# Channel-major conv history, taps and y without turns on TensorE, and early conditioning slabs in twos

## What is computed

```python
mod = silu(c) @ w_ada + b_ada            # 9 conditioning rows, 6 x 2048 columns
h = rmsnorm(x, norm1_g) * (1 + scale1) + shift1
qa, ka, va, qb, kb, vb, r, glr = split(h @ w_in)
x = x + gate1 * merge_out(mix_a(qa, ka, va), mix_b(qb, kb, vb), r) @ w_out
h2 = rmsnorm(x, norm2_g) * (1 + scale2) + shift2
g_pre, u = split(h2 @ w_up)
gp = concatenate([state_conv, g_pre])    # 2 old rows for each sample, zeros for the prompt
conv = conv_b + conv_w[0]*gp[0:T] + conv_w[1]*gp[1:T+1] + conv_w[2]*gp[2:T+2]
y = x + gate2 * ((silu(conv) * u) @ w_down)
new_conv = gp[T:]                        # the last 2 rows, an output
```

## Time and profile before

| what | value |
|---|---|
| median of 3 runs | 1593.41 us (1593.29 to 1593.66) |
| span of the profiled execution | 1592.4 us |
| TensorE matmul busy | 1569.0 us, 99% |
| VectorE, ScalarE busy | 899.9 us, 665.7 us |
| DMA moved | 371.06 MB, mean 233 GB/s |

### The profile page before, as it was taken

The page is one execution under the profiler, slowest core; times in us unless marked ns, Lnnn a source line. Parts: engine busy times, 40 slices in busy tenths (PEclk is TensorE's granted clock), DMA queues, the critical chain, the costliest instruction groups (busy, mean ns, idle before and its releaser), DMA issues.

```text
span 1592.4 us, 29203 instructions
## 1 busy us (share of the span) xinstructions
PE 1569.0 (99%) x12242; PEld 1418.5 (89%) x12242; DVE 899.9 (57%) x1525; ACT 665.7 (42%) x935; POOL 74.4 (5%) x131
## 2 busy tenths in 40 slices
PE   8999999999999999999999999999999999999997
PEld 4777888888888658888899999999999999999997
DVE  3555776656667536447454545545454566656663
ACT  3433444434446335325333333333333445545552
POOL 2000000001111000000000000000000000000000
PEclk8999999999999999999999999999999999999999
DMA  9999877777778998988844444454545554555460
GB/s 338 387 366 329 303 263 265 254 269 242 243 261 297 390 398 300 330 321 302 284 159 161 161 161 160 160 185 142 181 164 171 166 162 147 191 157 191 146 192 20
DMA packets 239232, 371.06 MB, mean 233 GB/s; under 512 B 7793, under 2 KB 188371, under 8 KB 230905
## 3 DMA queue, kind: packets, MB, share of 16 engines
q1 hardware_dynamic: 231888, 351.19, 63.8%
q0 software_dynamic: 7152, 17.90, 3.4%
q10 hardware_dynamic: 66, 0.14, 0.0%
HBM read 359.32 MB, written 9.88 MB: 232 GB/s over the span
## 4 chain that ended last, share of the span: by engine, by line
PE 84%; DMA 5%; issue 5%; DVE 3%; SPq 2%; ACT 2%; POOL 0%; ACTq 0%; POOLq 0%; DVEq 0%
PE ps L1046 24%; PE ps L1047 23%; PE ps L1048 23%; PE ps L998 3%; PE ps L1289 2%; DMA ring<-in_w_in 2%; PE ps L991 1%; DMA proj<-in_cache_v_win 1%; DMA vals<-in_w_ada 1%; SPq L610 1%; DMA ring<-in_w_out 1%; DVE wlo L2173 1%; PE ps L1360 1%; PE ps L1329 1%; ACT whi L1608 1%
## 5 line engine op out<-in xcount | busy, mean ns | idle before, releaser
L1046 PE MATMUL ps<-hhi,whi 128*128 128x288 f32 x3120 | 929.7, 298 | 1.5 <-DVE wlo L2014 0.5
L1047 PE MATMUL ps<-hlo,whi 128*128 128x288 f32 x3120 | 917.1, 294 | 0.0
L1048 PE MATMUL ps<-hhi,wlo 128*128 128x288 f32 x3120 | 917.0, 294 | 0.0
L1046 PEld LDWEIGHTS ps<-hhi,whi 128*128 128x128 f32 x3120 | 585.3, 188 | 43.6 <-issue 33.9
L1047 PEld LDWEIGHTS ps<-hlo,whi 128*128 128x128 f32 x3120 | 585.6, 188 | 0.7
L1048 PEld LDWEIGHTS ps<-hhi,wlo 128*128 128x128 f32 x3120 | 585.4, 188 | 0.0
L2014 DVE TENSOR_TENSOR wlo<-ring,whi 128x1024 fp32r<-128x1024 f32 x178 | 212.2, 1222 | 89.2 <-ACT whi L1599 88.8
L1599 ACT ACTIVATE whi<-ring 128x1024 fp32r<-128x1024 f32 x178 | 184.2, 1056 | 155.0 <-PE ps L1048 148.4
L2173 DVE TENSOR_TENSOR wlo<-ring,whi 128x1024 fp32r<-128x1024 f32 x96 | 117.0, 1222 | 84.6 <-ACT whi L1608 84.4
L1608 ACT ACTIVATE whi<-ring 128x1024 fp32r<-128x1024 f32 x96 | 100.8, 1053 | 145.6 <-PE ps L1048 112.3
L2695 DVE TENSOR_TENSOR wlo<-ring,whi 128x1024 fp32r<-128x1024 f32 (+1 forms) x94 | 105.7, 1132 | 56.0 <-ACT whi L1935 56.0
(11 more groups left out here) (323 smaller groups left out, 1141.5 us busy)
## 6 DMA issues: line engine op xcount, KB each, us to landing
ring<-in_w_up SPq DMA_DIRECT2D x88, 1024.0 KB, 5.2
ring<-in_w_ada SPq DMA_DIRECT2D x64, 1024.0 KB, 7.6
ring<-in_w_in SPq DMA_DIRECT2D x48, 1024.0 KB, 8.1
ring<-in_w_down SPq DMA_DIRECT2D x32, 1408.0 KB, 6.7
proj<-in_w_ada SPq DMA_DIRECT2D x28, 1024.0 KB, 9.4
ring<-in_w_out SPq DMA_DIRECT2D x16, 1024.0 KB, 8.6
ring<-in_cache_k_win SPq DMA_DIRECT2D x12, 1024.0 KB, 8.5
proj<-in_cache_v_win SPq DMA_DIRECT2D x8, 1024.0 KB, 13.1
```

The lines of the kernel that those rows point to most:

```text
L1046: mm(out, w_hi, x_hi, start=start, stop=False)
L1047: mm(out, w_hi, x_lo, start=False, stop=False)
L1048: return mm(out, w_lo, x_hi, start=False, stop=stop)
```

## The change

- `state_conv` is handed over as tiles of channels, once 128 x 704 numbers (360 KB), loaded by one DMA of GpSimd at the place of the first history load. VectorE copies from there to `gpad`. The history transposes are gone, and so are the 10 later loads.
- The last taps of all 11 turns are kept in SBUF (`last_taps`, in the place of `gates`) and stored by one DMA after the last turn. Their transposes, ScalarE's copies and 22 stores are gone.
- y is stored channel-major from `yst`, two tiles to a DMA of GpSimd. The row transposes and the copies to rows are gone. In the last chunk the even tile's 9 products come before the odd tile's 9; `last_out` works on each tile by itself, ScalarE stores the even one and SyncE the odd one. SyncE waits for all stores at the end.
- The first 22 entries of `ADA_AT` change from 0, 1, 2, 3, ... to 1, 1, 3, 3, ..., 21, 21. The last two stay behind chunk 22. The turns stay behind chunks 4, 8, 12, 16, 20 and 23. SyncE's order of loads, sorted by the same numbers, comes out the same.

```diff
+        last_taps = gates[:, 0:KF * 18].rearrange("p (n c) -> p n c", n=KF)
+        history = tail[:, 128:128 + KF * 16].rearrange("p (n b r) -> p n b r", n=KF, b=NB)
...
-        ADA_AT = [*range(22), 22, 22]
+        ADA_AT = [s // 2 * 2 + 1 for s in range(22)] + [22, 22]
...
-            sp.wait_ge(first_row_out, 1)
-            sp.dma_start(o["y_p"][0:P, 1536:2048], yrow[0]).then_inc(y_end_out, 16)
+            sp.wait_ge(*DE.upto("u", 0))
+            sp.dma_start(o["y"][:, 15], yst[:, 3]).then_inc(last_odd_out, 16)
+            for s, n in ((conv_out, 16), (k_out, 256), (v_out, 256), (stp_out, 64), (s0_out, 128), (y_out[0], 64),
+                         (y_out[1], 48), (last_even_out, 16), (last_odd_out, 16)):
+                sp.wait_ge(s, n)
...
             pool.wait_ge(*OL.upto("l3"))
-            pool.dma_start(hrow[:, 0], hist[:, 0:512]).then_inc(hist_in[0], 16)
...
+            pool.dma_start(history.rearrange("p n b r -> p (n b r)"), a["state_conv"].rearrange("p n c -> p (n c)")
+                           ).then_inc(hist_in, 16)
+            pool.wait_ge(*FV.upto("last", 10))
+            pool.dma_start(o["new_conv"], last_taps).then_inc(conv_out, 16)
+            for i in range(4):
+                for h in range(2 if i < 3 else 1):
+                    pool.wait_ge(*DV_.upto(f"u{h}", i))
+                    pool.dma_start(o["y"][:, 4 * i + 2 * h:4 * i + 2 * h + 2], yst[:, 2 * h:2 * h + 2]
+                                   ).then_inc(y_out[h], 16)
...
-            def up_turn(i, par):
-                pe.wait_ge(hist_in[par], i * 8 + (16 - 8 * par))
-                pe.wait_ge(*FV.upto("hist", i - 1))
-                pe.sem_inc(row_turns, 1)
-                for n in range(4):
-                    last = turn(ps[:, 4, 16 * n:16 * n + 16], hrow[:, par, P * n:P * n + P], ident[0:16, 0:16])
-                last.then_inc(*FT.step("hist"))
+            def up_turn(i):
...
-                pe.wait_ge(*FV.upto("last", i))
-                pe.wait_ge(*FA.upto("rows", i - 1))
-                for n in range(4):
-                    last = turn(ps[0:18, 5, P * n:P * n + P], glast[:, n, :], ident)
-                last.then_inc(*FT.step("rows"))
...
-            def row_turns_of(i):
...
-                        last = turn(ps[0:m, 4 + t, P * b:P * b + P], yst[:, b, P * t:P * t + m], ident)
-                    last.then_inc(*DT.step(f"t{t}"))
...
+                            end = i == 3 and j == 23
+                            order = [(k, n) for k in range(nk) for n in range(2)]
+                            for k, n in sorted(order, key=lambda kn: kn[1]) if end else order:
...
+                                if end and (k, n) == (nk - 1, 0):
+                                    last.then_inc(last_even_done, 1)
...
-                act.wait_ge(*FT.upto("rows", i))
-                act.wait_ge(conv_stored, i + 1)
-                f(crows, ps[0:18, 5, :], ACT.Copy).then_inc(*FA.step("rows"))
...
-            last_rows()
+            act.wait_ge(*DV_.upto("u1", 3))
+            act.dma_start(o["y"][:, 14], yst[:, 2]).then_inc(last_even_out, 16)
...
-                dve.wait_ge(*FT.upto("hist", i))
+                dve.wait_ge(hist_in, 16)
                 v.tensor_copy(gpad[:, :, 2 + SEQ:GW].rearrange("p n (b t) -> p n b t", t=6)[:, :, :, 0:2],
-                              ps[:, 4, 0:64].rearrange("p (n b r) -> p n b r", n=4, b=NB)).then_inc(*FV.step("hist"))
+                              history[:, 4 * i:4 * i + 4]).then_inc(*FV.step("hist"))
...
+                def last_out():
+                    dve.wait_ge(y_out[1], 48)
+                    dve.wait_ge(last_even_done, 1)
+                    dve.wait_ge(*DV_.upto("u0", 3))
+                    gated(5 * KD, 14, ps[:, 2:3, :], lambda m: yst[:, 2, :], DV_, 1, 3)
+                    dve.wait_ge(used, 3 * 24 + (CH_DOWN + BUFS + 24))
+                    dve.wait_ge(*DV_.upto("u1", 3))
+                    gated(5 * KD, 15, ps[:, 3:4, :], lambda m: yst[:, 3, :], DE, 0, 0)
```

More of the change, by code:

```diff
@@ L903, in _ @@
[L903 to L915, removed]
@@ L1936, in down_hi @@
                   ACT.Copy).then_inc(hi_done, 1)
[L1938 to L1951, removed]
-                act.wait_ge(*DT.upto("t2", 3))
-                f(yrow[2], ps[0:NS, 6, :], ACT.Copy).then_inc(third_row_out, 1)
-                act.wait_ge(third_row_out, 1)
-                act.dma_start(o["y_s"][:, 1536:2048], yrow[2]).then_inc(y_end_out, 16)
             def down_turn(i, end):
@@ L2544, in _, with gated @@
             head_lo(1)
-            def gated(gate, tile, psum, out, steps, n, i, end=False):
-                tmp = tmp_s[:, 64 * (n % 2):64 * (n % 2) + 64]
-                ts = tmp.rearrange("p (n b t) -> p n b t", n=2, b=NB)
-                gs = modT[:, bass.ds(tile + gate, 2), 1:NC9].rearrange("p n (b a) -> p n b a", a=1)
+            def gated(gate, tile, psum, out, steps, n, i):
+                c = psum.shape[1]
+                tmp = tmp_s[:, 64 * (n % 2):64 * (n % 2) + NS * c]
+                ts = tmp.rearrange("p (n b t) -> p n b t", n=c, b=NB)
+                gs = modT[:, bass.ds(tile + gate, c), 1:NC9].rearrange("p n (b a) -> p n b a", a=1)
+                first, last_step = (f"s{n}", f"u{n}") if steps is not DE else ("s", "u")
                 v.tensor_tensor(ts, psum[:, :, SEQ:TOK].rearrange("p n (b t) -> p n b t", t=TS),
-                                gs.to_broadcast([P, 2, NB, TS]), ALU.mult).then_inc(*steps.step(f"s{n}"))
-                for m in range(2):
-                    last = v.scalar_tensor_tensor(
+                                gs.to_broadcast([P, c, NB, TS]), ALU.mult).then_inc(*steps.step(first))
+                for m in range(c):
+                    v.scalar_tensor_tensor(
                         out=out(m)[:, 0:SEQ], in0=psum[:, m, 0:SEQ],
@@ L2558, in gated @@
                         op0=ALU.mult, op1=ALU.add)
-                if end:
-                    last.then_inc(last_shown, 1)
-                dve.wait_ge(*steps.upto(f"s{n}", i))
-                for m in range(2):
+                dve.wait_ge(*steps.upto(first, i))
+                for m in range(c):
                     last = v.tensor_tensor(out(m)[:, SEQ:TOK], tmp[:, NS * m:NS * m + NS],
                                            xT[:, bass.ds(tile + m, 1), SEQ:TOK].rearrange("p a c -> p (a c)"), ALU.add)
-                last.then_inc(*steps.step(f"u{n}"))
+                last.then_inc(*steps.step(last_step))
             def out_tiles(n):
```

126 lines of the change are left out of this document (39 added, 87 removed).

## The result

The changed kernel takes 1570.34 us (median; 1569.77 to 1571.64), the one before 1593.41: ratio 0.9858, 95% interval 0.9844 to 0.9872, faster by 23.1 us. The profiled span fell by 24.2 us, from 1592.4 to 1568.2; the median lies 1.0 us above this span before and 2.1 us after, which is why the two gains are not equal (more on that under the sum of the terms).

The account below looks back on a forecast made before the run. TensorE was taken as the bound, with DMA a second limit in the early input projection and single steps at the end; 10.4 + 4.6 + 1.75 - 0.7 + 2.5 = 18.5 us off gave 1574.9, range 1571 to 1579.

Parts of the forecast that it names:

- History and tap transposes: Borders between up projection turns: removing these transposes from TensorE saves 10.4 us, bounds 9.4 to 10.8.
- Rows of y: Down projection: removing the row transposes of y from TensorE saves 4.6 us, bounds 4.4 to 4.7.
- Slabs in twos: Early input projection: pairing conditioning slabs behind chunks saves 1.75 us after a load-bound wait, bounds 0 to 3.6.
- The bracket before chunk 3: Input projection: chunk 3 still starts at 59.65, so TensorE's wait there grows from 0.2 to some 1.8 us.
- Rival C: TensorE's waits before chunk 3 and at the value slab don't bind: 21 us off, 1572.4; chance 0.08.
- Rival B: Input projection: bunched slabs starve TensorE where DMA is full; 1597 us at 2.2 us per pair; chance 0.04.
- the lone turn: Input projection: a turn without a slab beside it, taken at 0.90 us; by the skill page's rule 0.79.
- The history load: Sample stage: one 360 KB load, 295 KB more, lengthens the DMA chain; -0.7 us, bounds 0 and 1.5 lost.
- the granted clock at 1.00: Sign in the profile after: TensorE's clock stays at 2.4 GHz behind both waits, before chunk 3 and at the value slab.
- The end: Final stores: last store issued sooner by SyncE and landing faster than GpSimd's; gain 2.5 us, bounds 1.9 to 3.7.
- The 4.75 I keep: Program's exit: the 4.75 us from the last store's landing to the end of the span stay unchanged.
- Rival D: Stores at the end take as long as before, since the end is the program's exit: 1577.4 us; chance 0.08.

Follow-up runs that it names:

- Experiment 11: Changed kernel with eight extra transposes of the last taps behind each of the 11 up projection turns, into an unread bank: 1579.93 us, ratio 0.9923.
- experiment 7: Changed kernel with the first four early conditioning slabs in twos behind chunks 1 and 2: 1567.32 us, ratio 0.9843.
- experiments 9 and 10: Changed kernel with its history load issued behind the sample stage: 1568.24 us; the same plus the first four slabs behind chunks 1 and 2: 1567.62 us.
- experiment 1: Changed kernel with the nine final waits for all stores moved from SyncE back to the end of GpSimd's program: 1570.79 us, ratio 0.9863.
- experiment 5: Two kernels: changed one with final waits on GpSimd and 30 more GpSimd transfers, 1573.23 us; kernel before with GpSimd's history loop written out, 1592.86 us.
- experiment 3: Kernel before with its seven final waits for all stores moved from GpSimd to SyncE: 1590.94 us, ratio 0.9986.
- experiment 2: Changed kernel with the last odd tile stored by GpSimd instead of SyncE, final waits still on SyncE: 1570.33 us, ratio 0.9855.

## Why the prediction was right in most terms and wrong in one

**History and tap transposes (10.4):** right. TensorE is 2.0 us ahead at the first product of the up projection and 12.2 behind its last turn, so the stage gave 10.2. Experiment 11 puts eight transposes back at every turn and pays 9.6.

**Rows of y (4.6):** right by the trace, not tested alone. TensorE's lead grows from 12.2 us ahead of the down projection's first border to 16.8 at its last product, 4.6. The sum of this and the term above is 14.8 measured, 15.0 forecast.

**Slabs in twos (1.75):** right in mechanism and about right in size: 1.6 at the turn ahead of chunk 23 (154.62 before, 153.03 after) and 1.9 at the last input product (496.40, 494.48). Undoing it alone gave 1.5 and 0.8 at those places and 1.0 by medians, so 1 to 2. The bracket before chunk 3 was 1.37 and not 1.8. Rival C said that the wait before chunk 3 doesn't bind; its bracket of 1.37 and experiment 7 say that it does. Rival B has no bracket between chunks 4 and 22. The Trainium skill ("TensorEngine Tiling (Array Packing)", Key Properties) has a drain for a change of the tiling mode and not for a change of tile alone. From that the prediction drew 0.79 for the lone turn. It cost 0.89, so the row was the better guide; whether the 0.10 more is a drain, no run shows.

**The history load (-0.7):** mis-sized. Against the kernel before it cost 0.1 in the stage (82.45 to 82.57 us). Four profiles of the kernel before and its variants spread over 82.08 to 82.59, six of the changed one at full clock over 81.75 to 82.88, so no cost is seen, and 0.7 can't be excluded by this alone. The step that failed is "The load grows from 2 x 33 KB to 360 KB, 295 KB more, / 408 GB/s = 0.72 us, all of it on the chain": the price of the change went by bytes. The load itself seems to have a price, 0.3 to 2.0 us (experiments 9 and 10). If that is so and the change cost nothing, the two small loads had cost about as much; that is an inference, no run took them out of the kernel before. How a small load comes to cost this stays open. The forecast also had the granted clock at 1.00 behind the waits; that holds in the changed kernel's profile but not in experiment 11's.

**The end (2.5; measured 7.4):** this is the term that put the time below the range, and its failing step is "The 4.75 I keep". The store came 0.71 us after VectorE's start (0.83 forecast) and landed 1.8 us later (2.2 forecast). These two parts give 2.03 + 1.0 = 3.0. The 4.75 was treated as a constant of the program's exit. It was 4.40 of GpSimd's DRAIN and some 0.4 of the rest, and the rest is what remains (1567.8 to 1568.2). Of the 4.40, experiment 1 gives 1.6 to 1.7 to the waits' move to SyncE, and experiment 5 gives 2.8 to the 34 transfers that GpSimd no longer issues: 3.0 + 4.4 = 7.4. (The other way round, in the kernel before, the waits' move alone gave 2.3 us of the profile, experiment 3; then 2.1 are left for the transfers.) The Trainium skill ("DMA: Bandwidth & Descriptors", Anatomy of one DMA) gives the path from GpSimd 2.0 us and the bytes at 436 GB/s, by which a 147 KB store has an estimated 2.34 us; in experiment 2, where GpSimd issued this store, it landed after 2.0. The change had both edits in plain sight, a wait list under another engine and shorter GpSimd code, and I gave neither a price. Rival D (2.5 less) erred to the other side. The range was too narrow for the same reason: even the sum of all the largest bounds, 10.8 + 4.7 + 3.6 + 0 + 3.7 = 22.8 us, ends at 1570.6, because the largest bound of the end was 3.7.

Summed up: terms 10.4 + 4.6 + 1.75 - 0.7 + 2.5 = 18.5; measured about 10.2 + 4.6 + 1.9 + 0.1 + 7.4 = 24.2 in the span. The 0.1 is the sample stage's -0.1, load included, and 0.2 between it and the up projection. The median fell 1.1 less than the span. A part is the spread of single executions (spans of the changed kernel were 1568.0 to 1570.1). Another part is time outside the span: in all the executions listed it is 1.5 to 1.7 us where GpSimd waits last and 1.5 to 2.0 where SyncE does, so that the move of the waits gives some 0.2 us back there.

## What to carry to other kernels

Before taking the end of a span as fixed, look up each engine's DRAIN: one that issues many transfers should finish its program early, and the final waits belong on an engine whose DRAIN is short. In a stage where DMA is full, don't price a small transfer by its bytes alone, and put it where DMA has room if that is free: it gave 2.1 us by medians in one kernel and nothing clear in another (experiments 9 and 10). Compare several profiles before reading a microsecond out of such a stage. A gain on TensorE ahead of a wait is lost up to the length of that wait, unless later work is moved into it (experiment 7).

## What the runs showed of the hardware that was not expected

- GpSimd's DRAIN at the end of the program: 1.62 us after 93 transfers, 4.07 after 123, 4.32 after 126, 4.40 after 127, all landed; 2.91 to 3.31 after 93 to 95 and 5.00 after 127 when it starts right behind a store. SyncE's takes 0.007 to 0.135 us.
- The same pair of waits in TensorE can leave the clock or bring it down. Behind 0.45 and 1.51 us, and behind 1.45 and 1.51, the granted clock fell from 2.4 GHz to the lower level (0.72 and 0.83 as the mean from 570 to 576 us); behind 0.49 and 1.53, and behind 0.20 and 1.51, it stayed at 1.00. Each fall cost 1.6 us by the rows. What decides, no run shows.
- Profiles of kernels that differ only behind the sample stage had 81.75 to 84.45 us in that stage and 385 to 399 GB/s in the same 25 us of it. A reading of 1 us or of 15 GB/s from one profile against one shows nothing there.
